# Two attention stages of a two-block transformer kernel: Gelu moved, score products joined, and VectorE's maxima set ahead of the previous difference

## The reference

```python
# first block
h = rms_norm(x, norm_mix_g);  z = h @ w_in
u, v = gelu(z[:, :512]), gelu(z[:, 512:1024])       # u and v of the gate
out_a = u * (masked sg_w @ layer_norm(v) + sg_b)    # spatial gate, 8 heads
out_b = softmax(q k^T / 8 + c_t - c_s, causal) v    # forgetting attention, 8 heads of 64
x = x + concat(out_a, out_b) @ w_out
x = x + conv_ffn(rms_norm(x));  x = rms_norm(x)
# second block
q, k, v, z, beta, g = parts of rmsnorm(x) @ w_in_2
o_dn = rmsnorm(gated_delta_rule(q, k, v, g, beta)) * silu(z)          # 4 heads, chunks
p0, p1 = softmax(q0 k0^T, causal), softmax(q1 k1^T, causal)           # two maps a head
o_df = rmsnorm((p0 - lam * p1) v) * silu(z)                           # 4 heads
x = x + concat(o_dn, o_df) @ w_out_2
```

## Time and profile before

| | us |
|---|---|
| median of three runs (lowest, highest) | 882.9 (882.83, 883.06) |
| profiled execution, its time | 882.26 |
| its span on the core | 880.6 |
| TensorE busy in the span | 870.3 |
| VectorE busy | 554.0 |
| ScalarE busy | 295.7 |

### The profile page before, as it was taken

How to read it: one execution, slowest core, us unless ns; L and a number is a source line. 1 busy time by engine, 2 the same in 40 slices (tenths; PEclk the granted TensorE clock), 3 DMA queues, 4 the chain that set the end, 5 groups by cost and what they waited for, 6 DMA issues and landing times.

```text
span 880.6 us, 13497 instructions
## 1 busy us (share of the span) xinstructions
PE 870.3 (99%) x4615; PEld 703.4 (80%) x4615; DVE 554.0 (63%) x978; ACT 295.7 (34%) x598; POOL 72.7 (8%) x138
## 2 busy tenths in 40 slices
PE   8999999999999999999999999999999999999998
PEld 7887767788888888888888888888788787678787
DVE  6258467374877777777744343478797573875654
ACT  7245476533222222222211010263331123555610
POOL 0000000010010011000000000010000000000000
DMA  8777433264655555556565655479655323221554
GB/s 277 235 225 234 140 130 120 97 192 159 223 191 191 191 191 192 191 191 196 194 195 195 194 194 198 160 246 280 199 173 155 120 98 97 96 96 48 192 195 141
DMA packets 53862, 154.74 MB, mean 176 GB/s; under 512 B 9628, under 2 KB 15020, under 8 KB 53688
## 3 DMA queue, kind: packets, MB, share of 16 engines
q1 hardware_dynamic: 24496, 75.84, 27.2%
q0 software_dynamic: 19008, 69.21, 24.2%
q10 hardware_dynamic: 10312, 9.06, 3.2%
HBM read 149.60 MB, written 4.49 MB: 175 GB/s over the span
## 4 chain that ended last, share of the span: by engine, by line
PE 92%; DVE 3%; ACT 2%; DMA 2%; issue 1%; SPq 0%; DVEq 0%; POOLq 0%; ACTq 0%
PE bank L753 80%; PE bank L1237 1%; PE bank L1215 1%; PE bank L941 1%; PE bank L917 1%; DMA RAW<-wstream 1%; PE bank L931 1%; DMA HI<-wstream 1%; ACT SQO L1712 1%; PE bank L1226 1%; PE bank L1126 0%; PE bank L1143 0%; DMA NCB<-out_t 0%; PE bank L794 0%; PE bank L1165 0%
## 5 line engine op out<-in xcount | busy, mean ns | idle before, releaser
L753 PE MATMUL bank<-GH,HI 128*128 128x512 f32 x708 | 284.0, 401 | 0.0
L753 PE MATMUL bank<-GH,LO 128*128 128x512 f32 x708 | 275.5, 389 | 0.0
L753 PE MATMUL bank<-GL,HI 128*128 128x512 f32 x708 | 275.1, 388 | 0.0
L1779 DVE TENSOR_TENSOR LO<-RAW,HI 128x1024 fp32r<-128x1024 f32 x86 | 105.2, 1223 | 108.5 <-DMA HI<-wstream 106.4
L753 PEld LDWEIGHTS bank<-GH,HI 128*128 128x128 f32 x708 | 133.0, 188 | 36.0 <-issue 8.7
L753 PEld LDWEIGHTS bank<-GH,LO 128*128 128x128 f32 x708 | 132.9, 188 | 28.1
L753 PEld LDWEIGHTS bank<-GL,HI 128*128 128x128 f32 x708 | 133.2, 188 | 24.3
L735 POOL DMA_DIRECT2D HI<-wstream x132 | 70.1, 531 | 783.8 <-PE bank L753 765.7
L1484 ACT ACTIVATE YC<-AB,PAR 128x512 f32<-128x512 f32 x44 | 36.1, 819 | 140.6 <-DVE AB L1966 140.6
L753 PE MATMUL bank<-AH,HI 128*128 128x512 f32 x176 | 68.5, 389 | 0.0
L753 PE MATMUL bank<-AL,HI 128*128 128x512 f32 x176 | 68.5, 389 | 0.0
(11 more groups left out here) (322 smaller groups left out, 1146.1 us busy)
## 6 DMA issues: line engine op xcount, KB each, us to landing
RAW<-wstream SPq DMA_DIRECT2D x135, 512.0 KB, 3.7
HI<-wstream POOLq DMA_DIRECT2D x132, 512.0 KB, 4.9
X<-x_t SPq DMA_DIRECT2D x8, 256.0 KB, 7.9
NCB<-out_t ACTq DMA_DIRECT2D x8, 256.0 KB, 4.0
out_t<-X ACTq DMA_DIRECT2D x8, 256.0 KB, 5.5
XR<-out_t ACTq DMA_DIRECT2D x8, 256.0 KB, 3.5
out_t<-XR SPq DMA_DIRECT2D x7, 256.0 KB, 5.3
EG<-out_t ACTq DMA_DIRECT2D x1, 1024.0 KB, 5.0
```

What stands on the lines that cost most here:

```text
L753: mm = pe.matmul(out, a, b, start=(first and n == 0), stop=(last and n == 2))
L1779: dve.tensor_tensor(LO[:, u % RING, :], RAW[:, u % RING, :], HI[:, u % RING, :].bitcast(F32), ALU.subtract).then_inc(unit_split, 1)
```

## The change

In mixer 1 TensorE's part of the scores gets an item of its own, `S`. For the steps i = 2 of pairs 1 to 3 (S 6, S 10, S 14) it stands right behind the weights-by-values product `C` (or the gate behind it), elsewhere right ahead of `A`; `_glued` keeps such neighbours free of filling. The first Gelu (three tiles) moves from behind `B` 7 to behind the scaling `N` 5.

In mixer 2 every slot becomes A n, D n - 1, C, B n - 2, so VectorE's maxima of a slot stand ahead of the last slot's difference; the last step becomes B 13, A 15, D 14. The second map is computed first (c = 0 is now the second map; it goes into `PB`, which gets two buffers, and the first into `P0`, which gets four), and the difference takes its reciprocal after the first exponential alone. The scores of step 0 move up to behind a sum of squares (`qk_sums`). One eighth of `z` stands ahead of `C` 3 and no longer in the scan. The new state is announced head by head. The norm's terms move from `difference` to item `C`, and the ring's subtraction for unit 130 moves from behind the fourth to behind the eighth part of the last `z`.

```diff
 def _first_step_inside(slots):
-    slots[-4] = [("D", 14), ("B", 13), ("A", 15)]
+    slots[-4] = [("B", 13), ("A", 15), ("D", 14)]
     slots[-3] = [("B", 14), ("D", 15), ("sb", 0)]
+    slots[-1].insert(0, ("P", 5))
...
     for n in range(NB * heads + 3):
         slot = []
+        if n < NB * heads:
+            slot.append((score, n))
         if 1 <= n <= NB * heads:
             slot.append((weigh, n - 1))
-        if n < NB * heads:
-            slot.append((score, n))
...
         slot = [("A", n)] if n < 16 else []
+        if n < 16 and (n % 4 in (0, 3) or n == 2):
+            slot.insert(0, ("S", n))
...
-            slot += [("C", n // 4 - 1), ("split", n // 4 + 3)]
+            slot += [("C", n // 4 - 1)] + ([("S", n + 1)] if n < 16 else []) + [("split", n // 4 + 3)]
...
+def _glued(items):
+    groups = []
+    for what, n in items:
+        if groups and (what in ("gate", "gelu") or (groups[-1][-1][0], what) in (("S", "A"), ("C", "S"), ("gate", "S"))):
+            groups[-1].append((what, n))
+        else:
+            groups.append([(what, n)])
+    return groups
...
     slots = _pairs()
+    slots[5].append(("gelu", 0))
     slots[9].insert(slots[9].index(("C", 1)) + 1, ("gate", 0))
-    slots[11].insert(1, ("gate", 1))
+    slots[11].insert(2, ("gate", 1))
...
-            + part(8, 12, [("gelu", 0)] + last[:8])
+            + part(8, 12, last[:8])
...
-        elif what == "z" and n[1] == 3:
+        elif what == "z" and n[1] == (7 if n[0] == 7 else 3):
             out.append(("ring", U_Z + n[0] + RING - 1))
...
-    + _with_products(_first_step_inside(_last_norms(_attention(4))), _eighths(range(5))[1:38], [])
-    + _merge(_eighths(range(4, 6))[6:13],
+    + _with_products(_first_step_inside(_last_norms(_attention(4))), _eighths(range(5))[1:39], [])
+    + _merge(_eighths(range(4, 6))[7:13],
...
             def scan_state(i):
-                pe.wait_ge(st_made, i)
...
                 for h in range(4):
+                    pe.wait_ge(st_made, 4 * (i - 1) + h + 1)
                     mm = pe.matmul(PS[6][:, blk(h)], KT[:, h, blk(i)], ST[:, h, :], start=True, stop=True)
...
+                    if n == 8 and part:
+                        df_scores(0)
...
-                        if c == 0 and n >= 3:
-                            act.wait_ge(dpt_mm, n - 2)
-                        if c == 1 and n >= 1:
-                            act.wait_ge(dw_made, n)
-                        act.activation(P0[:, n % 3, 0:w] if c == 0 else PB[:, 0:w], scores_of(n, c), ACT.Exp,
+                        if c == 0 and n >= 2:
+                            act.wait_ge(dw_made, n - 1)
+                        if c == 1 and n >= 4:
+                            act.wait_ge(dpt_mm, n - 3)
+                        act.activation(P0[:, n % 4, 0:w] if c else PB[:, n % 2, 0:w], scores_of(n, c), ACT.Exp,
...
+                dve.wait_ge(dexp, 2 * n + 1)
+                then(dve.reciprocal(rc, sums[:, i, 0:1]))
                 dve.wait_ge(dexp, 2 * n + 2)
-                then(dve.reciprocal(rc, sums[:, i, 1:2]))
-                then(dve.scalar_tensor_tensor(S1[:, 0:1], sums[:, i, 0:1], NEGLAM, rc, ALU.mult, ALU.mult))
+                then(dve.scalar_tensor_tensor(S1[:, 0:1], sums[:, i, 1:2], NEGLAM, rc, ALU.mult, ALU.mult))
```

## The result

The changed kernel took 886.98 us (median of 6 runs, 885.53 to 889.14) beside 882.87 (881.91 to 883.57) for the kernel before: a ratio of 1.0051, 95% interval 1.0042 to 1.0061, so 4.5 us slower, 3.7 to 5.4. The forecast was 884.8, range 882.2 to 886.2: the sign was right, the time lies outside. The profiled execution took 887.62, its span 885.8.

A forecast was written before the change was run, and what follows sets the result against it. TensorE, busy 870.3 of 880.6 us, was taken as the bound. Mixer 1's -0.8 and mixer 2's +2.75, taken as +1.9, put the profiled 882.26 at 884.2 and the median at 884.8, range 882.2 to 886.2.

The forecast's parts named there:

- wait at S 7: Mixer 1: the moved Gelu and its table loads delay step 6's exponentials, so TensorE waits at S 7, +1.5 us.
- Mixer 1: -2.4 + 1.5 - 0.7 + 0.8 = -0.8.: Mixer 1's sum: wait at step 8 gone, wait at S 7, three joined scores, time given back at S 12 and later.
- The joins: Mixer 1: three score groups right behind `C` each save a way in and out of filling, together -0.7 us.
- B 7 ... I take 1.0, and the same at B 11: Mixer 2: VectorE's chain to the difference takes 6.2 us against TensorE's 5.1; waits of 1.0 each, +2.0.
- B 14 ... +1.8: Mixer 2, last step: the difference of 14 comes behind step 15's maxima, so TensorE waits, +1.8 us (1.4 to 2.1).
- B 3 +0.3: Mixer 2: `B` 3 already waits 1.1 us; four maxima ahead of the difference add +0.3 (0 to 1.3).
- The subtraction for unit 130 ... -0.35.: End of mixer 2: moved behind the last eighth, it no longer delays norms; TensorE reaches og 6 earlier, -0.35 us.
- Scores of step 0 ... -0.2: Mixer 2: placed behind the sum of squares, they save one way in and out of filling, -0.2 us.
- This goes: -2.4: Mixer 1, step 8: TensorE's waiting behind the Gelu's old place, between gate product and filling, disappears, -2.4 us.
- the state by heads: Mixer 2's scan: the first product at `sa` 3 starts after one of four parts, -0.6 us (-0.8 to -0.2).
- the first (VectorE keeps up): Rival: no wait at `B` 7 and `B` 11, 882.8 us, chance 0.18; with `B` 14 covered too 881.0, 0.07.
- The third: Rival: waits chain through restart costs, `B` 3 meets all four maxima (+1.0), the scan gives nothing; about 886.2 us, chance 0.13.

The follow-up runs named there:

- a1: The changed kernel run again unaltered: 887.11 us, ratio 1.0049 to the kernel before.
- e7: Changed kernel with VectorE's difference ahead of the maxima again and the joined scores undone (every S right ahead of its A): 880.34 us, ratio 0.9979 to the kernel before.
- e1: Changed kernel with VectorE's difference of the last slot ahead of the maxima again, everywhere: 881.53 us, ratio 0.9992 to the kernel before.
- e8: Changed kernel with difference first, first Gelu ahead of step 4's copy, unit 131's subtraction behind og 5, and no joined scores: 878.02 us, ratio 0.9954 to the kernel before.
- e10: e9 with VectorE's maxima ahead of the last slot's difference again, in all slots and the last step: 880.95 us, ratio 0.9987 to the kernel before.
- e9: e8 with joined scores kept and ring subtractions of z products 1 to 3 behind the sixth eighth: 877.18 us, ratio 0.9943 to the kernel before.
- e11: Changed kernel with one line other, the first Gelu ahead of the copy of step 4: 885.73 us, ratio 1.0031 to the kernel before.

## Why the prediction was wrong, step by step

The mechanism that decides, maxima ahead of the difference make TensorE wait at `B` 7, 11 and 14, was right in place and in length, and so was the sign. The time was 2.2 above the forecast, outside the range. The step that failed is the pricing of the waits and savings around it. The table puts the forecast's terms beside what a1 lost or won against the kernel before, by place, both profiles at full clock:

| stretch | forecast | measured |
|---|---|---|
| S 6 joined | -0.2 | -0.1 |
| wait at S 7 | +1.5 | +1.7 |
| wait at `B` 8 gone, S 10 joined | -2.6 | -2.7 |
| S 12 | +0.5 | +0.55 |
| S 14 joined, `B` 13 | -0.2, +0.3 | -0.2, +0.7 |
| transfer that the reordering of tokens waits for | 0 | +0.3 |
| scores of step 0, `B` 0 | -0.2 | -0.1 |
| `B` 1 to `B` 14 | +4.1 | +4.55 |
| `B` 15, `C` 3 and the scan | -0.8 | -1.0 |
| behind the last z | -0.35 | +0.4 |
| the whole span | +1.9 | +4.1 |

1. *"Mixer 1: -2.4 + 1.5 - 0.7 + 0.8 = -0.8."* It came to -0.1: +0.7. The joins saved 0.5 (the rows that the forecast names give 0.18 each and 0.54 for three, not 0.7). But they brought 0.9 of the 1.7 that S 7 loses (e7 against e1), and all of the 0.7 at `B` 13, for which I had 0.3. So they were worth 0 where S 7 doesn't wait (e8) and cost 1.1 where it does (e7).
2. *"B 7 ... I take 1.0, and the same at B 11", "B 14 ... +1.8", "B 3 +0.3".* The idle times came as forecast at `B` 7, 11 and 14 (0.98, 0.99, 1.72); `B` 3 waits less (0.86, where 1.07 was before), and `B` 1 waits 0.29, which I had not seen. But a wait costs TensorE some 0.2 more than its idle time, 1.21 for 0.98 in the rows of e1 and a1: +0.45 for my 4.1. Against e1 the order costs 4.9: some other part of the change, all of which I had at nothing there, wins 0.4 in this stretch when the order is the old one (0.3 of it at `B` 3). Which part wasn't taken apart.
3. *"The subtraction for unit 130 ... -0.35."* VectorE got free earlier and waited for unit 131: 0 in the first profile and +0.4 in a1, as the transfer landed. I had named the transfer as a bound of 0.5; it was the bound already. *"Scores of step 0 ... -0.2"*: 0.3 are won there, but a small product soon behind them (L1073) then comes later by 0.3 in a1 and by 0.9 in e1, where the list shows it waiting for ScalarE (0.7).
4. *The clock.* No step and no rival had it. It was lower in 5 of 12 executions, which took 1.7 longer: 0.7 in the mean, 0.5 in the median (886.98 over all, 886.5 at full clock).

Of the 2.2 that the median missed, the clock is 0.5. Of the other 1.7, 0.7 are mixer 1, 0.45 the order, and 0.35 the end, which won nothing. The pair of profiles in the table misses 2.2 even at full clock, with the transfer's 0.3 and the 0.4 at the end, which both differ from execution to execution. So the last few tenths can't be given to a term.

What stood: *"This goes: -2.4"* at `B` 8, +0.5 at S 12, the state by heads (-0.7 for -0.6), and for the eighth of z about nothing: the wait at `C` 3 gone (0.69), that at `sb` 2 grown from 0.2 to 0.9. Of the rivals, the first (VectorE keeps up) is what e10 nearly makes true by hand at `B` 7 and `B` 11, where 0.4 each are left. The third, about 886.2 and given 0.13, came nearest in number; of its conditions the restarts came, but not the +1.0 at `B` 3, and the scan did give something.

Not settled: what decides whether the clock falls behind a given wait. The fastest kernel that came out is e9, 877.18, 0.57% (0.43 to 0.71) under the kernel before, though e8's interval overlaps its own: the difference first, the Gelu ahead of the copy of step 4, the subtraction of unit 131 behind og 5 and those of z's first rings behind the differences.

## What to carry to other kernels

Price a wait of the bound engine as its idle time plus the overlap that it breaks (here 0.2 us each). Where two halves of a step wait for a result each, count both: the list of waits showed 1.09 and 0.28 where 1.7 and 0.7 were lost. And ask of every wait of a microsecond or more whether the clock may fall behind it. Where a reordering puts an engine's result behind more of its queue, count all that stands ahead of it: here a subtraction of 1.2 us that nobody needed yet stood in three of the four long waits, and could be moved by itself, at the price of what then stood behind it. Compare profiles place by place: the difference of two whole spans held unrelated waits of half a microsecond and more. Two edits that look separate can carry each other (the Gelu's place and the joined scores): undo them singly and together before pricing either.

## What the runs showed of the chip that was not expected

- TensorE's granted clock fell to 0.50 for about 3.4 us behind single waits of 1.1 us (S 7, in the first profile and not in that of a1) and 1.7 us (`B` 14, in the profile of e11 and not in those of a1 and e10), 1.7 us lost each time. With the wait of 3.6 us (S 10) it was lower in all twelve executions, with that of 1.45 at `B` 8 of the kernel before in none of 65.
- A table load cost 1.29 and 1.30 until the next activation's start at both switches (112.05 to 113.34, 115.03 to 116.33): the figure of the load that the Trainium skill gives ("ScalarE: Activation LUTs", What ACT_TABLE_LOAD costs), without the drain that it adds.
- A row of the timeline that merges two matmuls can hide a wait: the row of 1.05 us at S 7 is two products of 0.50 that start 0.57 apart, each when its own exponential is done, and not one slow pair.
